# Copying two sets of weights within DRAM during the first mixer, and reading them from there in 8 KB rows

## What is computed

```
for i in range(DEPTH):                       # DEPTH = 2
    h = rms_norm(x, norm_mix_g[i])
    y = mla_mixer(h, ...) if i == 0 else fox_mixer(h, fox_w_in, ...)   # fox: z = h @ w_in, w_in is 2048 x 8208
    x = x + y
    h = rms_norm(x, norm_ffn_g[i])
    x = x + peer_ffn(h, peer_w_q[i], peer_sub_keys[i], peer_u[i], peer_v[i])

# peer_ffn: q = x @ w_q (2048 x 2048), scores against sub_keys, top 16 of 128 twice, top 16 of 256 pairs,
#   8 heads x 16 = 128 experts per token
u_sel = u[i_blk]                             # 128 rows of 8 KB per token
a = gelu(einsum('tkd,td->tk', u_sel, x_blk)) * g_blk
out = einsum('tk,tkd->td', a, v[i_blk])      # 128 more rows of 8 KB per token
```

## Time and profile before

| | us |
|---|---|
| median of 3 runs | 3493.96 |
| lowest and highest | 3489.74, 3494.89 |
| profiled execution, its own time | 3489.76 |
| its span, first to last instruction | 3487.9 |

### The profile page before, as it was taken

How to read it: one execution, slowest core, us unless ns; L and a number is a source line. 1 busy time by engine, 2 the same in 40 slices (tenths; PEclk the granted TensorE clock), 3 DMA queues, 4 the chain that set the end, 5 groups by cost and what they waited for, 6 DMA issues and landing times.

```text
span 3487.9 us, 26775 instructions
## 1 busy us (share of the span) xinstructions
PE 2807.9 (81%) x7404; PEld 1300.4 (37%) x7404; DVE 2079.6 (60%) x3766; ACT 900.7 (26%) x2304; POOL 1360.6 (39%) x1046
## 2 busy tenths in 40 slices
PE   7889967776778888888888788998888866766776
PEld 6444434443324333333333333443433322222222
DVE  4562677666677455545564755545555567777675
ACT  4341122221222123224121322332422222222221
POOL 4000355665555222223242522222234255555554
PEclk9999989999989999999999999999999988888888
DMA  4423899999999999999999999999999999999998
GB/s 145 158 99 121 337 414 416 416 415 410 421 407 420 417 417 417 417 417 419 417 410 418 406 417 417 417 417 417 417 416 408 418 413 419 421 419 418 414 419 356
DMA packets 239510, 1339.10 MB, mean 384 GB/s; under 512 B 27089, under 2 KB 48145, under 8 KB 105745
## 3 DMA queue, kind: packets, MB, share of 16 engines
q0 software_dynamic: 147456, 1073.81, 74.4%
q1 hardware_dynamic: 91920, 263.73, 19.6%
HBM read 1335.36 MB, written 2.10 MB: 383 GB/s over the span
## 4 chain that ended last, share of the span: by engine, by line
DMA 66%; PE 20%; DVE 6%; issue 5%; POOL 2%; ACT 1%; DVEq 0%; ACTq 0%; SPq 0%; POOLq 0%
DMA room<-in_peer_v_dram,index 62%; PE psum L1123 11%; DMA room<-in_peer_u_dram,index 4%; PE psum L989 2%; PE psum L1177 1%; PE psum L934 1%; POOL room L711 1%; PE psum L1013 1%; PE psum L750 1%; DVE resid L2155 1%; POOL room L723 1%; DVE room L2143 0%; PE psum L794 0%; PE psum L768 0%; PE psum L796 0%
## 5 line engine op out<-in xcount | busy, mean ns | idle before, releaser
L1123 PE MATMUL psum<-room,diag 128*128 128x512 f32 x3008 | 1573.3, 664 | 629.7 <-DMA room<-in_peer_v_dram,index 596.4
L2143 DVE CUSTOM_DVE_ANT_0 room<-room,normed 128x2048 f32<-128x2048 f32 x512 | 1172.8, 2291 | 659.7 <-DMA room<-in_peer_u_dram,index 651.8
L1123 PEld LDWEIGHTS psum<-room,diag 128*128 128x128 f32 x3008 | 584.4, 207 | 1545.6 <-issue 1256.6
L723 POOL DMA_INDIRECT room<-in_peer_v_dram,index x512 | 744.0, 1453 | 1033.7 <-PE psum L1123 992.3
L711 POOL DMA_INDIRECT room<-in_peer_u_dram,index x512 | 575.2, 1123 | 1041.8 <-DVE dots L2143 577.9
L1177 PE MATMUL psum<-wbuf,normedT 128*128 128x512 f32 x1536 | 694.2, 595 | 0.0
L1531 ACT ACTIVATE acts<-dots 128x1 f32<-128x1 f32 x512 | 103.6, 202 | 1827.2 <-DVE dots L2143 1826.8
L2155 DVE SCALAR_TENSOR_TENSOR resid<-room,acts,resid 128x512 f32<-128x512 f32 (+1 forms) x512 | 401.7, 785 | 285.2 <-DMA room<-in_peer_v_dram,index 284.9
L1177 PEld LDWEIGHTS psum<-wbuf,normedT 128*128 128x128 f32 x1536 | 284.6, 190 | 328.7 <-issue 325.6
L1540 ACT ACTIVATE diag<-ident,acts 128x128 f32<-128x128 f32 x512 | 205.5, 401 | 49.4 <-ACT acts L1535 2.6
L1535 ACT ACTIVATE acts<-acts,gates 128x1 f32<-128x1 f32 x512 | 150.9, 295 | 16.7
(11 more groups left out here) (224 smaller groups left out, 1687.4 us busy)
## 6 DMA issues: line engine op xcount, KB each, us to landing
wbuf<-in_fox_w_in_dram SPq DMA_DIRECT2D x128, 1024.0 KB
wbuf<-in_fox_w_o_dram SPq DMA_DIRECT2D x32, 1024.0 KB
wbuf<-in_peer_w_q_dram SPq DMA_DIRECT2D x32, 1024.0 KB
wbuf<-in_peer_w_q_dram SPq DMA_DIRECT2D x32, 512.0 KB, 12.0
wbuf<-in_mla_w_in_dram SPq DMA_DIRECT2D x8, 1024.0 KB, 7.2
wbuf<-in_mla_w_kvb_dram SPq DMA_DIRECT2D x32, 256.0 KB, 3.5
room<-in_mla_w_o_dram SPq DMA_DIRECT2D x8, 1024.0 KB, 11.8
room<-in_peer_u_dram,index POOLq DMA_INDIRECT x512
```

The source lines that it names most:

```text
L723: pool.indirect_dma_start(v_ring[:, r, :], None, v_table, bass.IndirectOffsetOnAxis(index[:, number % 2, s:s + 1], 0)).then_inc(v_full[r], 16)
L1123: mm = pe.matmul(psum[:, q, :], diag[:, r, :], v_ring[:, r, q * TILE:(q + 1) * TILE], start=at == 0 or n == SOLO and q == PE_BANKS - 1, st ...
L2143: V.tensor_tensor_reduce(u_ring[:, r, :], u_ring[:, r, :], normed[:, b, :], 1.0, 0.0, ALU.mult, ALU.add, dots[:, r:r + 1]).then_inc(dot_do ...
```

## The change

ACT gets 21 DMA issues between `copy_kv(0)` and the loop over the groups. They copy within DRAM. Seven copy the columns of heads 1 to 7 of `peer_w_q[0]` (2 MB each, 14.7 MB) into `laid_q`, where a partition's 16 rows of 1 KB lie one behind the other as 16 KB. Fourteen copy 7 of the 8 column blocks of `fox_w_in` (4 MB each, 58.7 MB) into `laid_in`, where the two 4 KB pieces that a partition takes in one load lie side by side as 8 KB. Issues for the first are 128 x 16 pieces of 1 KB, for the second 128 x 8 pieces of 4 KB.

SP then loads heads 1 to 7 as two loads of 1 MB in rows of 8 KB, instead of four of 512 KB in pieces of 1 KB, and 56 of the 64 `fox_w_in` loads of each block in rows of 8 KB. SP waits for all of `q_laid` before head 1, and for all of `in_laid` before the first staged load. What is computed stays as it was. The bytes that go on chip stay as they were too; the copies add 73.4 MB read and 73.4 MB written.

```
+LAID = 7
+        laid_q = nc.dram_tensor("laid_q", (PHEADS - 1, P, KC * 2 * P), F32, kind="Internal").ap()
+        laid_in = nc.dram_tensor("laid_in", (8 * LAID, P, 2 * WIDE), F32, kind="Internal").ap()
...
+        def pq_loaded(h):
+
+            return 32 * (h // PQ_TILES + 1) + (32 if h % PQ_TILES == 0 else 0)
...
-                for q in range(4):
-                    sp.dma_start(pq_tile[:, r, 4 * q:4 * q + 4, :],
-                                 w[:, 4 * q:4 * q + 4, h * 2 * P:(h + 1) * 2 * P]).then_inc(pq_full[r], 16)
+                if h == 1:
+                    sp.wait_ge(q_laid, 16 * (PHEADS - 1))
+                for half in range(2):
+                    sp.dma_start(pq_tile[:, r, 8 * half:8 * half + 8, :].rearrange("p k n -> p (k n)"),
+                                 laid_q[h - 1][:, half * D:(half + 1) * D]).then_inc(pq_full[r], 16)
...
+            def stage_laid(job, m):
+                r = staged(job, m)
+                sp.dma_start(stage[:, r].rearrange("p c n -> p (c n)"), laid_in[m - M_IN]).then_inc(stage_full[r], 16)
...
+            sp.wait_ge(in_laid, 32 * LAID)
             for job in range(NB):
                 for g in range(2):
                     for t in range(4):
                         for e in range(8):
-                            stage_wide(job, M_IN + 32 * g + 8 * t + e, fw, e, t * D + g * WIDE)
+                            if 4 * g + t < LAID:
+                                stage_laid(job, M_IN + 32 * g + 8 * t + e)
+                            else:
+                                stage_wide(job, M_IN + 32 * g + 8 * t + e, fw, e, t * D + g * WIDE)
...
-                    pe.wait_ge(pq_full[r], 64 * (h // PQ_TILES + 1))
+                    pe.wait_ge(pq_full[r], pq_loaded(h))
...
                 copy_q(0)
                 copy_kv(0)
+                w = rows_view(peer_w_q[0])
+                for h in range(1, PHEADS):
+                    act.dma_start(laid_q[h - 1].rearrange("p (k n) -> p k n", k=KC),
+                                  w[:, :, h * 2 * P:(h + 1) * 2 * P]).then_inc(q_laid, 16)
+                fw = rows_view(fox_w_in[0])
+                for i in range(LAID):
+                    cols = slice(i % 4 * D + i // 4 * WIDE, i % 4 * D + (i // 4 + 1) * WIDE)
+                    for c in range(2):
+                        act.dma_start(laid_in[8 * i:8 * i + 8, :, c * WIDE:(c + 1) * WIDE].rearrange("e p n -> p e n"),
+                                      fw[:, c:KC:2, cols]).then_inc(in_laid, 16)
                 with act.Fori(0, mla.groups - 1) as g:
```

More of the change, by code:

```diff
@@ L379, in hybrid_encoder @@
         pq_full = [sem(f"pq_full{r}") for r in range(PQ_TILES)]
+        q_laid = sem("q_laid")
+        in_laid = sem("in_laid")
         axpy_done, queried = sem("axpy_done"), sem("queried")
```

## The result

The changed kernel takes 3777.2 us (median of five runs; 3774.7 to 3783.4), the kernel before 3493.5 (five runs). The ratio is 1.082, 95% interval 1.080 to 1.083: 284 us slower. The forecast was 3808 us, range 3625 to 3920.

What follows compares the result with a forecast made beforehand. The first mixer was taken as bound by PE and engine hand-offs, the part from 360 us by DMA packets. 3489.8 + 334 (ACT's hold) - 19.5 (new loads) = 3804, 3808 us with 4.2 for the median; range 3625 to 3920.

Steps and rivals of the forecast that it cites:

- ACT is held: Ahead of the group loop, ACT's issues wait until all but about two of the last copies are through.
- C: ACT not held, copies at half the load rate; 204 us run over into the full part: 3678 us. Chance 0.11.
- D: ACT not held, copies at the load's rate, fitting idle DMA time: 3490 or 3474 us. Chance 0.12.
- The size of the hold: Before the first mixer's groups, the whole mixer stands still while ACT is held: +334 us, 167 at the other end.
- a copy passes DRAM twice: Copies read and write DRAM, 421 GB/s for both together, so half the rate: 376 us instead of 188.
- rival B: ACT held, copies as fast as loads, so 167 us of hold: 3641 us. Chance 0.15.
- The last copies beside the first groups: Last two copies, 21 to 42 us of DMA time, run beside the first two groups at no cost; up to 42 uncovered.
- "a few us at most" for the clock: PE's clock after the halt, at the start of the mixer's groups, costs a few us at most.
- What the new shapes give back: In the DMA-full part, 8 KB rows save 11.3 us on staged loads and 8.2 on queries: -19.5 us.
- The correction by 1.016: DMA shares over 1 were put down to packets of two queues overlapping, so DMA times were divided by 1.016.
- SP's new waits cost nothing: SP's two waits for the copies end long before SP reaches them: cost nothing.
- Rival E: ACT held, pieces inside DRAM dearer than twice a load's price, 501 us: 3975 us. Chance 0.12.

Runs made afterwards that it cites:

- q_on_act: Against the kernel before: only the seven query copies, on ACT, with heads 1 to 7 read from them; fox_w_in loaded as before. 3529.4 us, ratio 1.011.
- pool_copies: The changed kernel with the same 21 copies issued on POOL, after its last piece of the latent products, instead of ACT. 3616.7 us, ratio 1.036.
- other_source: The changed kernel with old load shapes, nothing reading the copies, and the 14 copies' 4 KB pieces taken from peer_w_q[0] instead of fox_w_in. 3704.0 us, ratio 1.061.
- reads_only: The kernel before with loads in the new 8 KB shapes straight from the weight tensors (wrong columns), no copies. 3476.0 us, ratio 0.9953.
- small_pieces: The changed kernel with each of the 14 fox_w_in copies cut into four by columns, 56 copies in 1 KB pieces. 3830.3 us, ratio 1.097.

## Why the prediction was right, point by point

The time lies in the range, 31 us under the forecast, on the side and by the mechanism forecast. The steps:

- **ACT is held.** Right. I read it from SP's issues behind 2048 pieces, and ACT's queue behaves alike; after ACT was let go its queue still moved 8.75 MB (2.1 fox copies) in the changed kernel and 1.5 query copies in q_on_act, where I had two. Rivals C and D (ACT not held) are out. pool_copies shows that they were half right about another engine: POOL's queue takes all 21, and the time is then 3617 us, in the place where C had 3678.
- **The size of the hold.** 334 us forecast, 282.7 measured. The term mis-sized is the price of the copies: "a copy passes DRAM twice", so half the rate, with 421 GB/s, the most that any slice showed, as the limit of both together. The seven query copies went at about a load's price: 51 ns a piece, 46 us of DMA time in all, close to rival B's 43, where I had 87. The fox copies came out near twice a load's price, 306 ns against 2 x 164, but for another reason: other_source copies pieces of the same size at 324 GB/s, with 648 GB/s of traffic. So the rule was wrong, and half right by accident. With the fox copies at other_source's price the changed kernel would take an estimated 3690 us (its 3704 less the 14 that the new shapes give back): still in the range, but 118 us under the forecast. That the forecast came within 31 us is luck in that term. A bound from what a trace happened to reach is not a limit. The figure of the Trainium skill that I set beside it ("DMA: Bandwidth & Descriptors", section "Latency and other measured facts"), 207 to 214 GB/s, meets the fox copies (217) and not those from `peer_w_q` (324 in other_source).
- **The last copies beside the first groups, "at nothing"**, with 42 us if the cover is gone. Measured 16.0 us. The cover was DMA engines two thirds idle, but the mixer needs each of its loads soon after it is issued, and the copies stood beside them. SP's loads from 386 to 450 us, in the changed kernel:

```profile
  PE psum L953: 14.6, 2
...
DMA to landing us min/median/max: 3.0/13.9/16.6
```

PE waited 14.6 us for two of them. Its clock was 0.50 to 0.51 of full in the halt, 1.2 of 2.4 GHz, and 0.83 on average from 386 to 450 us; what of the 16 us is the clock's was not taken apart. So "a few us at most" for the clock is neither borne out nor refuted.
- **What the new shapes give back.** 19.5 us forecast, 13.7 measured between the traces, 16 by reads_only. Window 0 gave 7.1 of 8.2. Windows 1 to 3 gave 6.6 of 11.3, though the rate where staged loads run rose as computed, from 417 to 421 GB/s. reads_only has 7.4 us in the same place. Runs of one kernel lie 5 to 9 us apart, so of this rest I can't say more.
- **A small misreading.** I laid shares over 1 to packets of two queues that overlap; but the gathers alone show 100.9% and ACT's queue alone 101.3%, so one queue does it too. The correction by 1.016 moves no term by more than 6 us.
- **SP's new waits cost nothing.** Right: SP's first load of `laid_q` is issued at 659.5 us, 299 us after its place before, with everything long landed.
- **Rival E** (small pieces inside DRAM dearer than twice) did not come: the 1 KB pieces of the query copies cost 51 ns against 48.7 for a load. Only from `fox_w_in` do small pieces come near it: small_pieces runs at 184 GB/s, under half of the 417 of the staged loads.

## What to carry to other kernels

A transfer that nobody waits for still costs its issuer: behind 7 to 21 transfers of one or two thousand pieces each, ACT stands until all but about two are through, so bulk copies belong on an engine that has nothing to do, at a moment when it has nothing to do. Idle DMA share is no cover by itself beside a stage that loads small weights just in time; the cover is a stretch in which no one waits for a load. And work out what the best case would bring before paying for it: rows of 8 KB for pieces of 4 KB were worth 1% of the rate, all the new shapes together 16 us of 3490. Moving 15 MB at the right place got half of that, while moving 73 MB at the wrong place lost 284 us.

## What was not expected of the hardware

- Copies inside DRAM ran at 324 GB/s from `peer_w_q` in pieces of 4 KB, 204 ns each, against 164 for the load of such a piece; with 1 KB, 51 against 49 ns.
- The same copies from `fox_w_in` ran at 217 GB/s, and in 1 KB pieces at 184, while loads from it on chip cost 164 ns for 4 KB as anything else. Another tensor seen in rows of 32,832 bytes also copied slowly, at 235 GB/s against 315 to 319 with 32,768, but with the engines idle a quarter of the time, which those of the changed kernel are not. The mechanism is open.
- POOL took 21 transfers, 73 MB, within 68 us of its first issue, 48 of them standing; ACT's issue behind two transfers of 1024 pieces took 19 us each.
- While POOL issued a transfer of 2048 pieces, one small DVE instruction of 128x4 took 0.63 to 0.69 us instead of 0.16 or 0.17, until the issue was over, in all seven groups.
